# Two steps more between the making of the linear-attention strips' operands and their clusters, and two small spread multiplications widened to 128 rows

## The reference, cut to what matters

```python
# GLA, per head, both directions: decayed causal scores, then scores times values
b = jnp.cumsum(gc, axis=2)
diff = jnp.where(mask, b[:, :, :, None, :] - b[:, :, None, :, :], -jnp.inf)
a = jnp.einsum('bhid,bhjd,bhijd->bhij', qc, kc, jnp.exp(diff))
o = o_inter + jnp.einsum('bhij,bhje->bhie', a, vc)
...
# mLSTM, per head, both directions: running maxima of the gates
m_t = jnp.maximum(log_inter, jnp.max(log_d, axis=-1))
d = jnp.exp(log_d - m_t[..., None])
s = jnp.einsum('bhtd,bhsd->bhts', q_, k_) * d
```

## Time and profile before

| | us |
|---|---|
| median of 3 runs | 894.59 |
| lowest, highest | 894.54, 896.09 |
| the profiled execution, whole | 894.32 |
| its span, first to last instruction | 892.5 |
| TensorE busy | 869.2 (97%) |
| VectorE busy | 618.3 (69%) |
| ScalarE busy | 491.9 (55%) |
| moved | 161.91 MB, 181 GB/s |
| mean granted TensorE clock | 0.995 of full speed |

### The profile page before, as it was taken

How to read it: one execution, slowest core, us unless ns; L and a number is a source line. 1 busy time by engine, 2 the same in 40 slices (tenths; PEclk the granted TensorE clock), 3 DMA queues, 4 the chain that set the end, 5 groups by cost and what they waited for, 6 DMA issues and landing times.

```text
span 892.5 us, 14942 instructions
## 1 busy us (share of the span) xinstructions
PE 869.2 (97%) x5520; PEld 747.5 (84%) x5520; DVE 618.3 (69%) x986; ACT 491.9 (55%) x802; POOL 13.1 (1%) x26
## 2 busy tenths in 40 slices
PE   5999998999999999999999999999999999999996
PEld 2878776887788888899999998998888999999985
DVE  3578987889779878775555557766787755555575
ACT  4587776665565665574444444453755544444554
POOL 0010000000000000000000000000000000000001
PEclk9999999999999999999999999999999999999998
DMA  9954323345447776636555557354434865555531
GB/s 362 362 149 135 124 97 111 110 134 172 137 147 262 262 266 227 236 111 204 186 190 187 188 185 265 113 187 141 143 118 142 271 230 201 184 182 186 189 111 48
DMA packets 45266, 161.91 MB, mean 181 GB/s; under 512 B 5500, under 2 KB 5660, under 8 KB 45216
## 3 DMA queue, kind: packets, MB, share of 16 engines
q1 hardware_dynamic: 43200, 156.78, 51.7%
q0 software_dynamic: 1296, 3.78, 1.5%
q10 hardware_dynamic: 720, 0.65, 0.2%
HBM read 160.15 MB, written 1.05 MB: 181 GB/s over the span
## 4 chain that ended last, share of the span: by engine, by line
PE 79%; DVE 11%; ACT 5%; issue 3%; DMA 1%; SPq 0%; POOL 0%; POOLq 0%; DVEq 0%; ACTq 0%
PE bank L776 67%; DVE w_lo L1868 3%; PE bank L964 1%; ACT w_hi L1366 1%; PE bank L954 1%; DVE arena L2254 1%; PE bank L1262 1%; DMA arena<-in_early 1%; DVE small L1898 1%; ACT gx_more L1598 1%; PE bank L1082 1%; PE bank L1077 1%; PE bank L1284 1%; PE bank L912 1%; PE bank L971 1%
## 5 line engine op out<-in xcount | busy, mean ns | idle before, releaser
L1868 DVE TENSOR_TENSOR w_lo<-raw,w_hi 128x1024 fp32r<-128x1024 f32 x244 | 288.1, 1219 | 151.0 <-ACT w_hi L1366 150.6
L1366 ACT ACTIVATE w_hi<-raw 128x1024 fp32r<-128x1024 f32 x244 | 245.5, 1050 | 191.5 <-PE bank L776 160.7
L776 PE MATMUL bank<-w_hi,act_lo 128*128 128x512 f32 (+1 forms) x728 | 291.3, 400 | 0.3 <-DVE w_lo L1868 0.2
L776 PE MATMUL bank<-w_lo,act_hi 128*128 128x512 f32 (+1 forms) x728 | 283.0, 389 | 0.0
L776 PE MATMUL bank<-w_hi,act_hi 128*128 128x512 f32 (+1 forms) x728 | 282.7, 388 | 0.0
L776 PE MATMUL bank<-act_lo,w_hi 128*128 128x256 f32 x640 | 182.9, 286 | 1.9 <-DVE act_lo L1868 1.4
L776 PE MATMUL bank<-act_hi,w_hi 128*128 128x256 f32 x640 | 181.0, 283 | 0.0
L776 PE MATMUL bank<-act_hi,w_lo 128*128 128x256 f32 x640 | 181.0, 283 | 0.0
L776 PEld LDWEIGHTS bank<-w_lo,act_hi 128*128 128x128 f32 x728 | 137.1, 188 | 28.9
L776 PEld LDWEIGHTS bank<-w_hi,act_lo 128*128 128x128 f32 x728 | 137.3, 189 | 28.3 <-issue 1.4
L776 PEld LDWEIGHTS bank<-w_hi,act_hi 128*128 128x128 f32 x728 | 137.3, 189 | 26.4 <-issue 1.0
(11 more groups left out here) (272 smaller groups left out, 735.1 us busy)
## 6 DMA issues: line engine op xcount, KB each, us to landing
raw<-in_stream SPq DMA_DIRECT2D x278, 512.0 KB, 4.4
arena<-in_early SPq DMA_DIRECT2D x16, 512.0 KB, 10.8
res<-in_x SPq DMA_DIRECT2D x2, 512.0 KB, 4.3
arena<-in_ctx SPq DMA_DIRECT2D x2, 512.0 KB, 11.1
res<-in_x POOLq DMA_DIRECT2D x1, 1024.0 KB, 10.3
arena<-in_norm_final POOLq DMA_DIRECT2D x1, 512.0 KB, 4.2
arena<-in_ple_b POOLq DMA_DIRECT2D x1, 512.0 KB, 5.2
out<-arena ACTq DMA_DIRECT2D x2, 256.0 KB, 2.6
```

Of the source, the lines that this page charges most:

```text
L776: last = pe.matmul(o, left, right, start=start and m == 0, stop=stop and m == 2, skip_group_check=shared)
L1366: return act.activation(o, i, ACT.Copy)
L1868: return dve.tensor_tensor(o, x, hi.bitcast(F32), ALU.subtract)
```

## The change

Four edits move the clusters. On TensorE the first cluster of a head goes from step 5 to step 7 and the second from step 0 of the next head to step 2. ScalarE's copies go from five to seven steps after their number; VectorE's put of item 0 from six to eight, the other puts from five to six. `queries` and `expand` go one step later, and the list of steps gets one more (43 instead of 42), so that `woven` places some steps a piece earlier or later.

The other edits widen the two spread multiplications to all 128 rows. `pick` and `pick_r` are first filled with zeros (two GpSimd instructions at the start of its program, semaphore `pick_zero`, for which VectorE and ScalarE wait before they write the few rows that matter); the data operands `mg_x` and `mg_both` take all 128 rows, of which the added ones meet zeros.

```diff
@@ level_steps
-    for s in range(N_ITEMS + 6):
+    for s in range(N_ITEMS + 7):
...
-        if e == 2 and h > 0:
+        if e == 3 and h > 0:
             out.append(("queries", h - 1))
-        if e == 5 and h > 0:
+        if e == 6 and h > 0:
             out.append(("expand", h - 1))
@@ views
-        mg_x = arena[0:32, 10, 0:T]
+        mg_x = arena[:, 10, 0:T]
-        mg_both = act_hi[0:32 + GH, 6:8, T:2 * T]
+        mg_both = act_hi[:, 6:8, T:2 * T]
@@ gpsimd
+            pool.memset(pick[:, :], 0.0).then_inc(pick_zero, 1)
+            pool.memset(pick_r[:, :].bitcast(F32), 0.0).then_inc(pick_zero, 1)
             wait_cut(pool, UNIT["gk", 3])
@@ tensor
             def gla_level(s):
-                if e == 5 and h < GH:
+                if e == 7 and h < GH:
                     level_batch(h, 0)
-                elif e == 0 and h > 0:
+                elif e == 2 and h > 0:
                     level_batch(h - 1, 1)
...
-                        last = pe.matmul(psum[5][:, 16 * t:16 * t + 16], mg_x[:, t * P:(t + 1) * P], pick[0:32, :],
+                        last = pe.matmul(psum[5][:, 16 * t:16 * t + 16], mg_x[:, t * P:(t + 1) * P], pick[:, :],
...
-                    head = pick_r[0:32 + GH, h:h + 1].broadcast_to([32 + GH, P])
+                    head = pick_r[:, h:h + 1].broadcast_to([P, P])
@@ scalar
             def gla_level(s):
-                n = s - 5
+                n = s - 7
...
-                    act.activation(mg_x, psum[4][0:32, 0:T], ACT.Copy).then_inc(mg_rows, 1)
+                    act.activation(mg_x[0:32, :], psum[4][0:32, 0:T], ACT.Copy).then_inc(mg_rows, 1)
...
+                    act.wait_ge(pick_zero, 2)
                     hi_part(pick_r[0:32, :], ident[0:32, 0:GH]).then_inc(pick_ready, 1)
@@ vector
             def gla_level(s):
-                for n in (s - 6, s - 5):
-                    if 0 <= n < N_ITEMS and not PUT_AT[n][0] and (n % PER_HEAD == 0) == (n == s - 6):
+                for n in (s - 8, s - 6):
+                    if 0 <= n < N_ITEMS and not PUT_AT[n][0] and (n % PER_HEAD == 0) == (n == s - 8):
...
+                    dve.wait_ge(pick_zero, 1)
                     dve.tensor_tensor(pick[0:32, :], ident[0:32, 0:16], ident[0:32, 16:32], ALU.add).then_inc(pick_ready, 1)
```

More of the change, by code:

```diff
@@ L619, in build @@
                              "mg_mt", "mg_md", "mg_em"))
+        pick_zero = sem("pick_zero")
         pick_ready, mg_hi, mg_lo, mh_bc, mh_arg, mh_exp, mh_s, mh_sd, mh_num, mh_out = (
```

## The result

| | before | after |
|---|---|---|
| median | 894.50 us (6 runs) | 887.14 us (6 runs) |
| lowest, highest | 892.77, 896.09 | 886.61, 888.57 |
| the profiled execution | 894.32 | 886.61 |
| its span | 892.5 | 884.8 |

A forecast was written before the change was run, and what follows sets the result against it. TensorE's row and its gaps were taken as the bound. Gaps 5.02 plus clock 1.58 less head 3 waits 1.0 gave 5.6; spreads 1.0 made 6.6 us saved, a median of 888.0 us, range 886.3 to 891.2.

The forecast's parts named there:

- What bounds the kernel: Whole kernel: TensorE, busy 869.2 of 892.5 us, sets the length; an edit counts only through its row or gaps.
- Heads 0 to 2: TensorE's gaps ahead of the first clusters there go, covered several times over by the clusters' new places: 1.84 us.
- 1.0 us for both clusters together: Head 3: waits that remain or newly appear at its first and second clusters, taken as 1.0 us, from 0 to 2.5.
- 1.26 us for the new order: VectorE, head 3: a weight piece (1.13 us) and a put (0.13) no longer stand ahead of item 4's operands.
- 0.8 for ScalarE's earlier exponentials: VectorE's way to head 3: later ScalarE copies shorten its waits by 0 to 2 us, taken as 0.8.
- the cause I named as a possible addition: Second cluster of head 3: up to 1 us more if ScalarE is late, with four expand instructions among the exponentials.
- The clock: Behind head 3's gap: the lower clock, 1.2 GHz, that follows TensorE's standing still goes too, saving 1.58 us.
- The spreads: Spread multiplications and gate pick over 128 rows: gaps into and out of them go, 1.0 us, between 0 and 1.4.
- Given back: Rival, chance 0.07: VectorE can't follow at rope and attention, equal waits appear between 150 and 230: about 894 us.
- What would have shown it wrong: Signs: head 3 wait of 2 us, put waiting for line 1060, TensorE's 150 to 230 waits up over 1 us, spread keeping 0.43.
- The slower rival: Chance 0.05: item 5's put, in its cluster's step, makes VectorE wait for TensorE in each head: 896.6 us.
- the rival in which VectorE gets ahead: Chance 0.15: the copies' new place gives VectorE the full 2 us, head 3 has no wait: 886.9 us.

The follow-up runs named there:

- One_step: Kernel before with clusters and copies one step later instead of two; queries, expand, other puts, list length and spreads unchanged: 891.90 us against 894.61, ratio 0.9962.
- copies_only: Kernel before with only ScalarE's copies moved, seven instead of five steps after their number: 893.13 us, executed once.
- awake_short: Kernel before with 3 extra multiplications, results unused, in TensorE's standing time ahead of head 3's first cluster: 894.09 us, executed once.
- puts_later: Changed kernel with VectorE's puts of items 5 to 8 and 4 seven instead of six steps after their number: 888.13 us, executed once.
- list_only: Kernel before with the list of steps one longer (43) and queries and expand one step later, nothing else: 893.79 us, executed once.
- awake: Kernel before with 10 extra multiplications, results unused, ahead of head 3's first cluster: 898.11 us against 894.61, ratio 1.004.

## Why the prediction was right, and where its steps were off

The mechanism was right in its main steps: the gaps ahead of the first clusters, the low clock behind the longest and the price of the narrow spreads are gone. That the median came within 0.9 us of the forecast is in part luck, since several terms were too small and one, the loss behind the spreads, was missing, with the other sign.

**What bounds the kernel.** TensorE's row and its gaps: right. Its busy time fell by 5.4 us (869.2 to 863.8) although it executes the same 5520 instructions, in part since the time of the low clock had counted as busy.

**Heads 0 to 2.** 1.84 us expected, and no gap is left. One_step shows that half the shift was enough.

**Head 3.** The term "1.0 us for both clusters together" was too large: the first cluster waits not at all, the second 0.43. The mis-sized number under it is VectorE's way. I took 1.26 us for the new order and 0.8 for ScalarE's earlier exponentials, operands at 138.6. They came at 137.24; corrected for the earlier start (0.35), 1.0 us sooner than reckoned. The order was right (busy time 60.51 to 59.38, 1.13 us); VectorE's waits fell by 2.1 us, not 0.8. The 0.8 was a choice between 0 and 2, not worked out. By copies_only the copies alone are worth 0.86; more than half of the 2.1 us (1.1) appears only when the clusters and puts move too. The wait of 1.02 us for a rounded weight piece in head 2 of the kernel before, which I had not looked at, is gone, and the waits of 1.43, 1.43 and 1.44 us for exponentials became 0.73, 0.67 and 0.88.

The second cluster of head 3 was where I expected the next wait, and it is there, from the cause I named as a possible addition: ScalarE is late by 0.84 us, and four copies of `expand` (line 1611, 1.03 us) stand directly ahead of the last exponential (142.11). Without them being ahead there might be no wait; that wasn't tried.

**The clock.** 1.58 us expected, 1.58 measured by awake_short in the same nine starts.

**A term that was missing.** The first four multiplications of a cluster took 0.68 us behind a gap and 0.60 without one (`x4` in the earlier trace rows and above), the next started 0.61 and 0.54 us later: four times 0.07 is 0.3 us. With it the section adds up: 5.02 + 1.58 + 0.3 - 0.43 = 6.5, measured 6.49; predicted 5.6.

**The spreads.** 1.0 expected, 1.42 measured. The two gaps were right (0.08 expected and 0.09 measured, 0.20 and 0.20). I overlooked the third row of the same view: the block behind the narrow form takes 0.10 us longer. In heads 0, 2 and 3 this makes 0.39 us each. In head 1 the entry waited longer by 0.17 us, and at most 0.04 was left, where I had counted 0.20. The pick gave 0.28 instead of 0.15. Behind the last spread the gain didn't stay, as follows.

**Given back.** "After the section the gain should be kept" held from 152 to 570 us: `gsfirst`, the attention and the last multiplication ahead of the pick all come 6.8 us earlier. It didn't hold behind the last spread. TensorE, 8.25 us ahead of the kernel before when it leaves that spread, is 7.87 ahead from line 1265 on (1262 before), and keeps that to its last instruction. These 0.38 us are lost in every kernel with 72 or 128 rows (0.33 to 0.39), and none is lost with 36 or 64 (at most 0.02). ScalarE ahead of this multiplication, before:

```profile
640.08 0.63 ACT L1366 ACTIVATE act_hi<-arena 128x512 fp32r<-128x512 f32 x1 [1.10 <-DVE arena L2290]
640.62 0.67 ACT L1437 ACTIVATE arena<-bank,stat 128x512 f32<-128x512 f32 x1
```

ScalarE and TensorE of the changed kernel:

```profile
632.22 0.63 ACT L1369 ACTIVATE act_hi<-arena 128x512 fp32r<-128x512 f32 x1 [1.10 <-DVE arena L2294]
632.75 0.67 ACT L1440 ACTIVATE arena<-bank,stat 128x512 f32<-128x512 f32 x1
```

```profile
632.92 0.39 PE L779 MATMUL bank<-w_lo,act_hi 128*128 128x512 f32 x1
633.52 0.67 PE L1265 MATMUL bank<-arena 128*128 128x257 f32 x2 [0.22 <-issue]
```

The multiplication of line 1265 asks for the tile that ScalarE's line 1440 writes, and starts 0.10 us after its end at 633.42. Before, that copy ended at 641.29 and the multiplication started at 641.39, likewise 0.10 us later. So it waits for this copy in both kernels. The copy stands directly behind an instruction that waits 1.10 us for VectorE, again in both. All of VectorE's and ScalarE's instructions from 625 us on (before) up to this copy come 7.87 us earlier after the change, the lead that TensorE had behind the third spread; nothing in this chain waits for the last spread. TensorE gained 0.38 us more there and had to wait it off. So the last of the four widened spreads was worth nothing at the end, and the spreads and the pick together 1.42 - 0.38 = 1.04 us: that the forecast's 1.0 comes out is luck. This is "given back" in small, at a place that I hadn't looked at. It is read from the traces; no kernel moved that copy. The other 0.18 of the 0.56 us lie behind TensorE's last start, where the output is finished: 8.41 us after the change and 8.23 before. Over all kernels this tail is 8.23 to 8.34 us, and 8.39 to 8.41 in the three with both parts of the change; why is open.

**What would have shown it wrong.** One of the signs named there did appear: a put waits for the second cluster's line (1060, now 1063) in head 0, 0.53 us at 89.11. It was too strict a sign, since TensorE lost nothing by it. The others did not: no wait in head 3 is near 2 us, and TensorE's waits between 150 and 230 are 0.4 us in both kernels. The slower rival, which rested on just such waits, was refuted by puts_later. Of the rival in which VectorE gets ahead, the first half came true (2.1 us of waits freed, its condition was 2) and the second didn't, since ScalarE holds the last operands. The median, 887.14, lies between its 886.9 and the forecast's 888.0, and nearer to the rival's, though the wait in head 3 that it did away with is still there.

**The sum of the errors.** +0.57 (head 3), +0.3 (the broken-up clusters), +0.4 (the spreads) and +0.35 (the start, which is chance), against -0.56 (behind the spreads). With the 6.6 predicted that makes the 7.7 of the spans. The medians differ by 7.36 us, and the forecast for the median was off by 0.86.

## What to carry to other kernels

Where one engine is busy all the time and waits for operands in bursts, move the consumer until the work between covers how far the producer is behind, and reckon it for the last burst of a section by itself: there the gap was four times the others', with no more cover than the smallest of them, and there lay two thirds of the gain, the clock included. Look also at what the producer waits for: VectorE won 2.1 us from shorter waits for other engines and 1.1 from its own order. A multiplication over 36 rows between full ones costs 0.39 us here, and zeros up to 72 rows remove it; whether that reaches the end depends on the next engine with a fixed schedule, so look for it behind the place, too.

## What the runs showed of the hardware that I had not expected

- 64 rows cost what 36 cost and 72 what 128 cost; the change lies between, and part of its price (0.10 us) falls on the multiplications behind.
- The lower of the two clock levels, 1.2 GHz, came behind stands of 3.03 and 3.04 us (four kernels) and one of 2.57 us (one_step) and not behind one of 2.43 us (copies_only) or 2.42 us (list_only), with nearly the same work around them:

```profile
142.20:145.90 3.70, 3.70 (x46) 1.00 0.02 8
```

  This row is copies_only's (PE busy, granted clock, DMA share, GB/s). In one_step the eight starts from 142.46 on take 3.50 us, in list_only the same eight 1.94: 1.56 us that one gap cost and another, nearly as long, did not. What decides it these runs don't tell.
- A multiplication of 512 columns with plain float32 operands, as in awake, took 0.87 us (8.74 for 10, two instructions each), where those of the rounded weights start every 0.23 us.
- A gain on the busiest engine is lost where its next operand comes from a chain that didn't move: 0.38 us at line 1265, in each of the five kernels with the wide spreads and in none of the nine others.
